# Layer 1 attention makes and stores its output turned, with one GpSimd operation per unit that divides the probabilities

## What is computed

```python
def _gqa_axial(h, w_qkv, g_qn, g_kn, w_o, row, col):
    b, s, _ = h.shape
    proj = h @ w_qkv
    q = proj[..., :HB * HD].reshape(b, s, HB, HD)
    k = proj[..., HB * HD:(HB + KVB) * HD].reshape(b, s, KVB, HD)
    v = proj[..., (HB + KVB) * HD:].reshape(b, s, KVB, HD)
    q = _axial_rope(_rms(q, g_qn), row, col)
    k = _axial_rope(_rms(k, g_kn), row, col)
    o = _block_attention(q, k, v, HD ** -0.5)
    return o.reshape(b, s, HB * HD) @ w_o
```

## Time and profile before

| what | us |
|---|---|
| median of 3 runs | 2411.65 (2409.13 to 2412.7) |
| span of the profiled execution, first to last instruction | 2406.4 |
| PE busy in it | 2205.8 (92%) |
| DVE, ACT, POOL busy | 1613.7, 1261.6, 545.4 |
| mean granted TensorE clock | 0.957 of full |
| layer 1's attention: prologue, 8 groups | 1068 to 1155, 1155 to 1584 |
| output block of layer 1, up to its last projection | 1588 to 1779 |

### The profile page before, as it was taken

The page is one execution under the profiler, slowest core; times in us unless marked ns, Lnnn a source line. Parts: engine busy times, 40 slices in busy tenths (PEclk is TensorE's granted clock), DMA queues, the critical chain, the costliest instruction groups (busy, mean ns, idle before and its releaser), DMA issues. The chain is left out here.

```text
span 2406.4 us, 32340 instructions
## 1 busy us (share of the span) xinstructions
PE 2205.8 (92%) x11028; PEld 1677.9 (70%) x11028; DVE 1613.7 (67%) x1832; ACT 1261.6 (52%) x1486; POOL 545.4 (23%) x430
## 2 busy tenths in 40 slices
PE   8899998969999999977899999969969999999993
PEld 5677776747777777746788888757756777777772
DVE  3566664578888888855566566552258888888883
ACT  3444443157777777743443434341107777777772
POOL 1100000012234233205232222200000332344222
PEclk9999998979999999987999999989979999999997
DMA  7000004769999999934111112152169999999983
GB/s 264 1 14 8 13 14 156 280 228 378 385 385 378 396 382 383 351 95 135 36 49 49 49 48 61 56 191 88 70 245 342 382 381 389 390 380 383 393 295 126
DMA packets 169530, 520.40 MB, mean 216 GB/s; under 512 B 11808, under 2 KB 49440, under 8 KB 169184
## 3 DMA queue, kind: packets, MB, share of 16 engines
q1 hardware_dynamic: 162272, 494.05, 54.4%
q0 software_dynamic: 7168, 25.17, 4.5%
HBM read 481.43 MB, written 37.75 MB: 216 GB/s over the span
## 5 line engine op out<-in xcount | busy, mean ns | idle before, releaser
L1764 DVE TENSOR_TENSOR m_w_lo<-s_raw,m_w_hi 128x2048 fp32r<-128x2048 f32 x384 | 865.9, 2288 | 144.6 <-ACT m_w_hi L1713 143.0
L1713 ACT ACTIVATE m_w_hi<-s_raw 128x2048 fp32r<-128x2048 f32 x384 | 731.1, 1916 | 175.9 <-PE m_ps_down L1809 77.3
L1807 PE MATMUL m_ps_gate<-m_w_hi,m_xeT_hi 128*96 128x512 f32 x512 | 206.0, 402 | 3.8 <-DVE m_xeT_lo L1770 3.8
L1807 PE MATMUL m_ps_down<-m_w_hi,m_hidT_hi 128*96 128x512 f32 x512 | 203.9, 398 | 3.8 <-DVE m_hidT_lo L1770 3.8
L1809 PE MATMUL m_ps_gate<-m_w_hi,m_xeT_lo 128*96 128x512 f32 x512 | 204.3, 399 | 0.0
L1809 PE MATMUL m_ps_down<-m_w_hi,m_hidT_lo 128*96 128x512 f32 x512 | 204.1, 399 | 0.0
L1807 PE MATMUL m_ps_up<-m_w_hi,m_xeT_hi 128*96 128x512 f32 x512 | 203.9, 398 | 0.0
L1684 POOL DMA_INDIRECT acc<-m_ye,m_row_scatter x32 | 47.0, 1469 | 688.4 <-ACT m_ye L1730 688.4
L1809 PE MATMUL m_ps_up<-m_w_hi,m_xeT_lo 128*96 128x512 f32 x512 | 202.7, 396 | 0.0
L1808 PE MATMUL m_ps_gate<-m_w_lo,m_xeT_hi 128*96 128x512 f32 x512 | 202.5, 395 | 0.0
L1808 PE MATMUL m_ps_down<-m_w_lo,m_hidT_hi 128*96 128x512 f32 x512 | 202.3, 395 | 0.0
(11 more groups left out here) (228 smaller groups left out, 4200.4 us busy)
## 6 DMA issues: line engine op xcount, KB each, us to landing
s_raw<-in_w_gate SPq DMA_DIRECT2D x128, 1024.0 KB, 7.6
s_raw<-in_w_up SPq DMA_DIRECT2D x128, 1024.0 KB, 7.3
s_raw<-in_w_down SPq DMA_DIRECT2D x128, 1024.0 KB, 7.8
s_raw<-in_w_qkv_b SPq DMA_DIRECT2D x16, 512.0 KB, 5.8
s_raw<-in_w_qkv_b SPq DMA_DIRECT2D x32, 256.0 KB, 6.1
s_raw<-in_w_o_b SPq DMA_DIRECT2D x1, 8192.0 KB, 23.2
acc<-o_x SPq DMA_DIRECT2D x12, 512.0 KB, 2.6
xn<-o_xn SPq DMA_DIRECT2D x12, 512.0 KB, 3.0
```

The costliest lines, as they stand in the source:

```text
L1713: act.activation(hi[:, split, :, :].rearrange("p k n -> p (k n)"), raw[:, slot, :], ACT.Copy).then_inc(hi_ready, 1)
L1764: dve.tensor_tensor(lo[:, split, :, :].rearrange("p k n -> p (k n)"), raw[:, slot, :], hi[:, split, :, :].rearrange("p k n -> p (k n)"), A ...
L1807: pe.matmul(out[:, cols], left_hi[:, k, :], hi[:, split, kk, cols], start=(k == 0), stop=False)
```

## The change

The division by the row sums moves from the end (the output of a unit, L306) to the probabilities before they are turned: POOL multiplies the whole unit's probabilities with the reciprocals in one operation, in place. The probabilities are then turned, split in high and low by ACT and DVE, and PE makes the output directly in the turned form, with V as the stationary factor. ACT and DVE split that output, and it is stored turned and split, 256 KB a unit, in place of 768 KB a group. The output block loads a tile's turned high and low parts (2 MB) and multiplies; it has no transposes and no split of its own there, and two buffers for its result. The gains are no longer multiplied into the rotation tables: POOL multiplies them with the power of each tile instead (`scale`). Line numbers of the kernel after the change are other ones.

```diff
+class TurnedCore:
+    RING = 4
+    def pe_turn(self, pe, n, unit, ident):
+        _, nk = keys_of(unit)
+        pe.wait_ge(self.scaled, n + 1)
+        for j in range(2):
+            if j == 0:
+                wait(pe, self.pT_split, 2 * n - 1)
+            else:
+                wait(pe, self.oT_split, n)
+            for k in range(nk):
+                last = pe.transpose(self.T[:, j, k, :], self.probs[:, unit % 2, j, k * P:(k + 1) * P], ident)
+            last.then_inc(self.turned, 1)
+    def pe_pv(self, pe, n, unit, v_hi, v_lo):
+        key, nk = keys_of(unit)
+        pe.wait_ge(self.pT_split, 2 * n + 2)
+        out = self.oT[0:self.dv]
+        for k in range(nk):
+            pe.matmul(out, v_hi(key + k), self.pT_hi[:, k, :, :], start=(k == 0), stop=False)
+            pe.matmul(out, v_hi(key + k), self.pT_lo[:, k, :, :], start=False, stop=False)
+            last = pe.matmul(out, v_lo(key + k), self.pT_hi[:, k, :, :], start=False, stop=(k == nk - 1))
+        last.then_inc(self.pv_done, 1)
+    def act_high(self, act, n, unit):
+        _, nk = keys_of(unit)
+        wait(act, self.pv_done, n)
+        for j in range(2):
+            act.wait_ge(self.turned, 2 * n + j + 1)
+            act.activation(self.pT_hi[:, 0:nk, j, :], self.T[:, j, 0:nk, :], ACT.Copy).then_inc(self.pT_high, 1)
+    def act_out(self, act, n, ring):
+        act.wait_ge(self.pv_done, n + 1)
+        if not (isinstance(n, int) and n < self.RING):
+            act.wait_ge(self.stored[ring], n * 4 - ring * 4)
+        act.activation(self.out[0:self.dv, ring, :, 0, :], self.oT[0:self.dv], ACT.Copy).then_inc(self.oT_high, 1)
+    def dve_inverse(self, dve, n, unit):
+        dve.wait_ge(self.exp_done, 2 * n + 2)
+        wait(dve, self.scaled, n - 1)
+        dve.reciprocal(self.rinv[:, unit % 2, :], self.rowsum[:, unit % 2, :]).then_inc(self.rinv_done, 1)
+    def pool_scale(self, pool, n, unit):
+        _, nk = keys_of(unit)
+        pool.wait_ge(self.rinv_done, n + 1)
+        at = self.probs[:, unit % 2, :, 0:nk * P]
+        pool.tensor_tensor(at, at, self.rinv[:, unit % 2, :].unsqueeze(2).to_broadcast([P, 2, nk * P]),
+                           ALU.mult).then_inc(self.scaled, 1)
...
@@ gqa_block, sync @@
-            sp.wait_ge(tables_ready, 15)
             weights(1, 1, 0)
             weights(1, 1, 1)
+            store(GROUPS - 2, 0)
             sp.wait_ge(proj_done, NU * GROUPS)
             sp.dma_start(shared.w_o_b, io.w_o_b[0].rearrange("(k p) n -> p k n", p=P)).then_inc(shared.w_o_landed, 16)
-            core.store(sp, GROUPS - 2, 0)
-            core.store(sp, GROUPS - 1, 1)
+            store(GROUPS - 1, 1)
@@ gqa_block, gpsimd @@
                 pool.tensor_tensor(rstd[:, t % 2, :], mean[:, t % 2, :], half[:, :], ALU.pow).then_inc(rstd_ready, 1)
                 pool.wait_ge(rstd_ready, m + 1)
+                pool.tensor_tensor(scale[:, :, :], gains[:, :, :],
+                                   rstd[:, t % 2, :].unsqueeze(2).to_broadcast([P, 3, HD]),
+                                   ALU.mult).then_inc(scale_ready, 1)
+                pool.wait_ge(scale_ready, m + 1)
...
-            pool.wait_ge(tables_landed, 48)
-            for h in range(3):
-                table(h)
-                norm.pool_tile(pool, 2 + h, half[:, 0:1])
-            norm.pool_tile(pool, TILES - 1, half[:, 0:1])
-            pool.wait_ge(tables_ready, 5 * 3)
+            pool.wait_ge(tables_landed, 64)
             for t in range(TILES):
+                if t + 2 < TILES:
+                    norm.pool_tile(pool, t + 2, half[:, 0:1])
                 tile(t, t)
+            core.pool_scale(pool, 0, 0)
             with pool.Fori(1, GROUPS) as g:
                 for t in range(TILES):
+                    core.pool_scale(pool, g * NU - NU + t + 1, (t + 1) % NU)
                     tile(g * NU + t, t)
@@ gqa_block, vector @@
                 dve.tensor_reduce(ssq[:, t % 2, :], squares, AX.X, ALU.add).then_inc(ssq_ready, 1)
+                dve.wait_ge(v_ready, m + 1)
+                dve.tensor_tensor(V_lo[:, slot, t, :], core.proj[:, t % 2, 3 * HD:], V_hi[:, slot, t, :],
+                                  ALU.subtract).then_inc(v_split, 1)
...
-                    core.dve_copy(dve, n, unit)
-                    core.dve_rinv(dve, n, unit)
+                    core.dve_low(dve, n, unit)
...
                     if not last:
-                        squared(g * NU + NU + unit, unit)
+                        squared(g * NU + NU + unit, 1 - slot, unit)
                         if unit:
                             turned(g + 1, 1 - slot, unit - 1, core.proj)
-                    core.dve_out(dve, g, n, unit, slot, first or (isinstance(g, int) and g < 2))
+                    if not (last and unit == NU - 1):
+                        core.dve_inverse(dve, n + 1, (unit + 1) % NU)
+                    core.dve_out(dve, n, (slot * NU + unit) % core.RING)
@@ output_block @@
             def load_o(i):
+                if STORED_TURNED:
+                    wait(sp, y_done, 2 * i - 2)
+                    sp.dma_start(oT[:, i % 2, :, :, :].rearrange("p k c n -> p (k c n)").bitcast(F32),
+                                 io.oT_b[ORDER[i]].rearrange("p k n -> p (k n)")).then_inc(o_landed[i % 2], 16)
+                    return
...
-                        wait(pe, x_ready, 2 * i - 1 + n)
+                        wait(pe, x_ready, 2 * i - 3 + n if STORED_TURNED else 2 * i - 1 + n)
...
-                if i + 1 < TILES:
+                if i + 1 < TILES and not STORED_TURNED:
                     turn_o(i + 1)
```

More of the change, by code:

```diff
@@ L223, in pe_scores @@
         last.then_inc(self.scores_done, 1)
-    def pe_scores_of_parts(self, pe, n, unit, high, low, q_index, k_index):
-        wait(pe, self.exp_done, 2 * n - 2)
-        key, nk = keys_of(unit)
-        tile, _ = UNITS[unit]
-        keys = slice(key * P, (key + nk) * P)
-        for j in range(2):
-            queries, out = slice((tile + j) * P, (tile + j + 1) * P), self.S[:, unit % 2, j, 0:nk * P]
-            pe.matmul(out, high[0:self.dk, q_index, queries], high[0:self.dk, k_index, keys], start=True, stop=False)
-            pe.matmul(out, high[0:self.dk, q_index, queries], low[0:self.dk, k_index, keys], start=False, stop=False)
-            last = pe.matmul(out, low[0:self.dk, q_index, queries], high[0:self.dk, k_index, keys],
-                             start=False, stop=True)
-        last.then_inc(self.scores_done, 1)
     def pe_turn(self, pe, n, unit, ident):
@@ L998, in step @@
                     n = g * NU + unit
[L999 to L1005 removed]
+                    core.act_high(act, n, unit)
                     if not (last and unit == NU - 1):
@@ L1009, in step @@
                         projected(g + 1, 1 - slot, unit)
+                    if unit == 0:
+                        turned(g, slot, TILES - 1, core.proj)
+                    elif not last:
                         turned(g + 1, 1 - slot, unit - 1, core.proj)
+                    core.act_out(act, n, (slot * NU + unit) % core.RING)
                     if unit in (2, 4) and not (isinstance(g, int) and g >= GROUPS - 2):
```

232 lines of the change are left out of this document (158 added, 74 removed).

## The result

The changed kernel takes 2442.06 us in the median (2435.61 to 2444.14), the kernel before 2410.41 us (2409.13 to 2412.7) beside it on the same chip: a ratio of 1.0127, 95% interval 1.0111 to 1.0143. The profiled execution has a span of 2440.7 us where the one before has 2406.4, so the stages have 34.3 us to account for.

What follows compares the result with a forecast made beforehand. PE was taken to set the time in the groups and output block. Terms +64, +19, +13, -1.5, -9.5 and -32 sum to +53 on a span of 2406.4, giving 2459.4 and a median of 2464 us; range 2428 to 2498.

Steps and rivals of the forecast that it cites:

- The new loop: Seven projecting groups: PE's next turn waits for POOL's scaling, behind projection, DVE's sum and reciprocals; 9.1 us a group, +64 us.
- The clock: Projecting groups: PE idles before turns and its clock falls, nearly two falls a group at 1.4 us each; +19 us.
- Rival 1: Groups: the clock falls behind nearly every wait, 48 us instead of 19; 2495 us or above; chance 0.15.
- The last group: Last group, no projection: longer unit chains, output split and slower clock, +13 us; smaller last store, -1.5 us.
- the five steps: Last group: five steps from unit to unit, each 1.3 to 2.6 us longer, 8.5 us together.
- the predicted chain: Last group: turn, two ACT copies, exponentials, reciprocals, scaling in sequence; 6.1 us for a unit of 4 tiles.
- The prologue: Before the groups: POOL's table operations go, and with them PE's waits for normed rows and the half clock; -9.5 us.
- The output block: Output block: transposes, their waits and clock falls go, and the first tile starts earlier; -32 us.
- Rival 3: Groups: the scaling is hidden, by reciprocals early enough or a short operation; 2368 us if fully hidden; chance 0.05.

Runs made afterwards that it cites:

- experiment 2: The changed kernel with POOL scaling only the first 16 columns of each probability row, the rest left undivided: 2388.33 us, ratio 0.9904.
- experiment 3: The changed kernel with a second POOL scaling over half of the columns behind the first, with a wait between them: 2540.31 us, ratio 1.053.
- experiment 1: The changed kernel with the next unit's reciprocals moved ahead of the sum of squares in DVE's queue, in the seven projecting groups: 2378.38 us, ratio 0.9854.
- experiment 6: The changed kernel with the reciprocals one DVE operation earlier, ahead of the low part of q and k but behind the sum: 2419.97 us, ratio 1.0036.

## Why the prediction was right, and where its size was off

The sign, the place and the mechanism were right. The median came 22 us below the 2464 predicted, inside the range. By terms, in the profiled executions:

- **The new loop, +64.** Right in kind, too large by 17. Leaving out the six falls of the clock (9.4 us, each unit's length less that of its like), the seven groups take 451.7 us, 64.5 each, and 47 more than before. The scaling was taken at 2.3 us and 1.15, and is 1.89 and 1.04; over four large and two small ones in a group that is 1.9 us, 13 of the 17. The price per unit then reads 66.3 - 1.9 = 64.4, which is what the groups at full clock show (64.0 to 64.6). The other 4 us are the side of before: its seven groups average 57.8 us with the first, and I had multiplied the 57.2 of the earlier trace rows by seven. The low end of my bounds, 2.0 us, was above what came. The rows of the scaling's line give the reason (shortest, median and longest in ns):

```profile
L434 POOL TENSOR_TENSOR s_raw<-s_raw,b_rinv x48: 1038/1892/3007, 1149.5 to 1643.6; 128x1024 f32<-128x1024 f32 x32, 128x512 f32<-128x512 f32 x16
```

  1.038 us for 512 elements and 1.892 for 1024 are 1.67 ns an element and 0.18 us an operation (by which experiment 2's 32 elements would take 0.24 us, as they do), so that scaling a row of 384 elements up in proportion carried the fixed part along 2.7 times. On the page that I weighed, the Trainium skill, GPSIMD Engine Reference, section 3.1 (Elementwise — side-by-side cycle accounting), the estimate for this size was 2.25 us; the rows say 1.89, with one of the two inputs a broadcast factor, and the measurement decides.
- **The clock, +19.** 9.4 us: six falls in seven groups, 1.5 to 1.7 us each, where I had taken nearly two a group. Behind units 1 and 4 the waits are 1.8 to 2.0 us in place of 2.4, behind 2 and 3 they are 1.2 to 1.3 in place of 1.8, and behind 5 and 0 they are 1.1 and less. Only the longest were followed by a fall, in 6 of 14 cases. Rival 1 was one step away: experiment 3 made the waits 2.3 to 5 us, and then almost every one was.
- **The last group, +13 and -1.5.** 9.6 us, near the sum of 11.5, but in part by luck. From its first to its last turn the group grows by 8.9 us, where the five steps were put at 8.5. Of that 3.3 are its first unit (6.30 to 9.63 us), where PE waits 4.2 us, before 2.5, for a rotated tile that has no projection to hide behind, a wait that the prediction left out. The other four steps grow by 1.0 to 2.1 each. A unit of four key tiles takes 5.3 to 5.8 us; the predicted chain takes 5.40, with the scaling of 1.9 and not 2.3 in it (6.1 predicted with that). It isn't what PE waits for most: 8.4 us in 5 places go ahead of PV, for the low part of the turned probabilities, and 1.8 in 3 ahead of turns, for the scaling. Behind the last turn 0.7 us came, where the split, the slower clock and the store were put at 3.0 together. The page's DMA issues answer to the earlier trace rows: a store is 256 KB in place of 768, and lands in 2.1 us in place of 4.4.

```profile
oT_b<-b_out SPq DMA_DIRECT2D x48, 256.0 KB, 2.1
o_oT<-oT_b SPq DMA_DIRECT2D x6, 2048.0 KB, 9.7
```

- **The prologue, -9.5.** This step failed: 0.3 us lost, and 2.8 to 2.9 in experiments 1 and 6, whose prologue is the same. PE's last projection there does end earlier (the last turn of a row starts at 1145.33, before at 1149.19), but that is 3.9 us and not 9.5: between 1104.00 and 1136.00 the clock is 1.00 in place of 0.89, which is the 3.4 that I had put for it, while PE still idles 5.4 us where it idled 5.9. The two waits that make most of it before, 2.74 and 1.87 us, are for the low part of the turned rows, and they did not go with the tables. And what is won goes before the first turn of a probability: PE waits 6.8 us there for the first scaling, which takes 3.01 us beside the split of the weights, and before it waited 2.66 for ACT's exponential. I had named the bound "0 if another wait comes up", and had not looked for it. The rows of that wait, of POOL and then of DVE:

```profile
1149.52 3.01 POOL L434 TENSOR_TENSOR s_raw<-s_raw,b_rinv 128x512 f32<-128x512 f32 x1 [1.35 <-DVE b_rinv L427]
```

```profile
1149.28 0.17 DVE L427 RECIPROCAL b_rinv<-b_rowsum 128x2 f32<-128x2 f32 x1
1149.36 5.32 DVE L1148 TENSOR_TENSOR b_w_lo<-s_raw,b_w_hi 128x2048 fp32r<-128x2048 f32 x2
```

- **The output block, -32.** -31.8. The waits of the earlier trace rows are gone and PE is busy for 150.32 us without one once it starts; the one wait left is the load's at the start, with the first product 7.95 us behind the issue where 7.5 was predicted. (The median of the six loads is 9.7 us; the other five are hidden.)

The terms were off by -17, -10, -2 and +10: what came is 53 - 19 = 34. The prologue's error hid a third of the others. The rest of the 22 us is the step from the span to the median, 5.2 us before and 1.4 now. A run's own time lies 1.7 to 2.2 us above its span, so some 3 of the 5.2 were that the profiled execution of the kernel before was a quick one, and the prediction carried them along. Rival 3 gave 2368 us for a hidden scaling; experiment 1 hides it and takes 2378. The largest part of the 10 us between them is the prologue's failed term, which is 12 us off there; the last group, which loses 8.7 and not 5, adds some 4, and the groups, which gain 10.5 and not 7, take as much back. What it asked for, "reciprocals early enough", was one move in DVE's queue.

## What to carry to other kernels

Ask of an operation added between two engines not how busy its engine is but which instruction ahead of it in the queue it has to stand behind: here the reciprocals could have run some 4 us earlier (at 1268.87, when DVE fell idle, and not at 1272.84) and waited behind a sum that they had nothing to do with, and that alone turned a gain of 1.5% into a loss of 1.3%. Where such a step is in a closed loop each half microsecond counts in full, and the waits that it leaves can cost clock on top: 22 us for one swap of two DVE operations. Where it is out of the loop, even its engine is free to choose. Before an idle POOL is given work, look for what DVE does at that time.

## What the runs showed of the hardware that I had not expected

A POOL operation that starts with or just behind DVE's split of the weights (2.28 us, 2048 columns, both inputs in SBUF) takes about 2 us more, whatever it is: 2.97 for 0.85, 3.01 for 1.04, 3.04 for 1.04, 2.94 for 1.01, and 2.21 for the 0.24 of experiment 2. Its amount is the same for an operation on three columns as for one on 512, so it reads like standing still and not like half speed. It goes the other way too. In the kernel before POOL's operation at 1205.45 starts 0.06 us ahead of the split and takes its usual 1.03, and the split takes 3.12:

```profile
1205.51 3.12 DVE L1020 TENSOR_TENSOR b_w_lo<-s_raw,b_w_hi 128x2048 fp32r<-128x2048 f32 x1
```

```profile
1205.45 1.03 POOL L929 TENSOR_TENSOR s_raw<-b_normed,b_tables 128x384 f32<-128x384 f32 x1
```

So the one that comes second pays. The Trainium skill, GPSIMD Engine Reference, section 1 (Specifications), lists contention with VectorE instructions that have two SBUF inputs; the trace agrees, with those numbers. In the changed kernel this is hidden except in the prologue; in experiment 3 it was on the loop.

PE's clock fell to half (1.2 of 2.4 GHz; the eight transposes at 1275.02 above take 1.80 us where the ones at 1264.02 take 1.09) behind waits ahead of the turns of the seven groups: of 1.84 to 1.99 us in 6 of 14 cases in the changed kernel, of 2.28 us and more in 24 of 26 and of 1.88 and 1.91 in both cases in experiment 3, and behind 1.77 and less in none of the two, each fall costing 1.5 us of the unit. So 1.1 us more of waiting cost 2.6 in a unit, and 1.4 us of useless products in the wait gave 29 us back to the kernel. Length alone doesn't decide it: in the kernel before two of five waits of 2.46 us stayed at full clock, and the same prologue wait of 2.90 us was followed by full clock in the changed kernel and by a fall in experiment 6. Why the fall comes at one wait and not at the next stays open.
